# A two-layer fp32 trunk on one core: branch outputs turned by the DMA instead of TensorE, and a rearranged start

## The reference, cut to what matters

```
x = x + 0.5 * swiglu_ffn(rmsnorm(x), w_ffn1_in, w_ffn1_out)        # D_FF 2816
u = rmsnorm(x);  q,k,v,g,p,c,gates = split(u @ w_in)
y_ret  = (retention(q, k, v) * silu(g)) @ w_ret_out                # 4 heads of 128
y_pool = pool_mixer(p) * pool_scale
y_conv = silu(layernorm(depthwise_conv31(a * sigmoid(b)))) @ w_conv_out   # a, b = split(c)
merged = sig(g0)*y_ret + sig(g1)*y_pool + sig(g2)*y_conv
x = x + merged @ w_out
x = x + 0.5 * swiglu_ffn(rmsnorm(x), w_ffn2_in, w_ffn2_out)
```

## Time and profile before

| | us |
|---|---|
| median of 3 runs (range) | 1141.62 (1141.49 to 1142.49) |
| the profiled execution's own time | 1143.67 |
| its span, first to last instruction | 1141.7 |
| PE busy in the span | 1128.9 (99%) |
| DVE busy | 794.9 (70%) |
| ACT busy | 630.0 (55%) |

### The profile page before, as it was taken

How to read it: one execution, slowest core, us unless ns; L and a number is a source line. 1 busy time by engine, 2 the same in 40 slices (tenths; PEclk the granted TensorE clock), 3 DMA queues, 4 the chain that set the end, 5 groups by cost and what they waited for, 6 DMA issues and landing times.

```text
span 1141.7 us, 13153 instructions
## 1 busy us (share of the span) xinstructions
PE 1128.9 (99%) x5063; PEld 931.9 (82%) x5063; DVE 794.9 (70%) x974; ACT 630.0 (55%) x723; POOL 31.5 (3%) x68
## 2 busy tenths in 40 slices
PE   9999999999999999999999999999999999999997
PEld 6788888788878888888888888878888788888886
DVE  5756565799999766555476656477999986665543
ACT  6755536654555675644465554275637366655442
POOL 1000000000100000000000000000001001000000
PEclk9999999999999999999999999999999999999999
DMA  9976665663764586756587656475637646876541
GB/s 348 324 242 219 211 233 160 239 175 139 243 241 151 164 292 212 238 156 230 174 274 250 236 180 233 176 217 207 212 120 261 233 152 184 273 244 210 168 184 37
DMA packets 116078, 240.99 MB, mean 211 GB/s; under 512 B 84256, under 2 KB 85664, under 8 KB 91440
## 3 DMA queue, kind: packets, MB, share of 16 engines
q1 hardware_dynamic: 112512, 232.28, 60.8%
q0 software_dynamic: 1648, 6.06, 1.5%
q10 hardware_dynamic: 1856, 1.81, 0.5%
HBM read 219.16 MB, written 1.05 MB: 193 GB/s over the span
## 4 chain that ended last, share of the span: by engine, by line
PE 86%; DVE 7%; DMA 2%; ACT 2%; issue 2%; SPq 1%; POOLq 0%; DVEq 0%; POOL 0%; ACTq 0%
PE acc L385 28%; PE acc L387 28%; PE acc L386 28%; DVE w_lo L1172 3%; DVE y L1396 1%; DMA raw<-in_weights 1%; PE tr L477 1%; ACT w_hi L770 1%; DMA hT_planes<-h_planes 1%; SPq L708 1%; ACT pin L945 0%; DVE gates L1471 0%; DVE ua L1452 0%; DVE gates L1416 0%; DVE qk L1461 0%
## 5 line engine op out<-in xcount | busy, mean ns | idle before, releaser
L1172 DVE TENSOR_TENSOR w_lo<-raw,w_hi 128x2048 fp32r<-128x2048 f32 (+2 forms) x204 | 444.4, 2211 | 87.7 <-ACT w_hi L770 87.7
L770 ACT CAST w_hi<-raw 128x2048 fp32r<-128x2048 f32 (+2 forms) x204 | 375.2, 1849 | 230.0 <-PE acc L387 221.8
L385 PE MATMUL acc<-w_hi,xT_hi 128*128 128x512 f32 x1152 | 453.1, 393 | 1.3 <-DVE w_lo L1172 1.1
L387 PE MATMUL acc<-w_hi,xT_lo 128*128 128x512 f32 x1152 | 449.3, 390 | 0.0
L386 PE MATMUL acc<-w_lo,xT_hi 128*128 128x512 f32 x1152 | 449.1, 390 | 0.0
L385 PEld LDWEIGHTS acc<-w_hi,xT_hi 128*128 128x128 f32 x1152 | 216.7, 188 | 46.4 <-DVE w_lo L1172 1.5
L387 PEld LDWEIGHTS acc<-w_hi,xT_lo 128*128 128x128 f32 x1152 | 216.7, 188 | 45.6
L386 PEld LDWEIGHTS acc<-w_lo,xT_hi 128*128 128x128 f32 x1152 | 216.9, 188 | 43.9
L1248 DVE SCALAR_TENSOR_TENSOR h<-acc,rs,silu_gate 128x256 f32<-128x256 f32 x88 | 42.5, 483 | 154.7 <-ACT silu_gate L837 154.4
L385 PE MATMUL acc<-w_hi,hT_hi 128*128 128x512 f32 x348 | 135.4, 389 | 0.0
L386 PE MATMUL acc<-w_lo,hT_hi 128*128 128x512 f32 x348 | 135.4, 389 | 0.0
(11 more groups left out here) (138 smaller groups left out, 629.4 us busy)
## 6 DMA issues: line engine op xcount, KB each, us to landing
raw<-in_weights SPq DMA_DIRECT2D x192, 1024.0 KB, 5.0
raw<-in_weights SPq DMA_DIRECT2D x20, 256.0 KB, 7.2
raw<-in_weights SPq DMA_DIRECT2D x8, 512.0 KB, 3.5
bias<-in_gate_bias POOLq DMA_DIRECT2D x6, 512.0 KB, 6.5
x<-in_x SPq DMA_DIRECT2D x2, 512.0 KB, 10.7
hT_planes<-h_planes SPq DMA_TRANSPOSE x64, 3.1
scale_row<-in_pool_scale POOLq DMA_DIRECT2D x2, 512.0 KB, 7.7
x_first<-in_x_first ACTq DMA_DIRECT2D x7, 128.0 KB, 6.0
```

The costliest lines, as they stand in the source:

```text
L385: nc.tensor.matmul(o, a_hi, b_hi, start=first, stop=False)
L387: return nc.tensor.matmul(o, a_lo, b_hi, start=False, stop=last)
L770: nc.scalar.copy(w_hi[:, hf % HIGHS, 0:n], raw[:, hf % RAWS, 0:n]).then_inc(hi_split, 1)
L1172: nc.vector.tensor_tensor(w_lo[:, hf % RAWS, 0:n], raw[:, hf % RAWS, 0:n], w_hi[:, hf % HIGHS, 0:n].bitcast(F32), ALU.subtract).then_inc(l ...
```

## The change

- `u` and `merged` are no longer transposed by PE. ACT splits them into planes, SP issues a DMA transpose; for `u` ACT joins (`u_out`), for `merged` DVE joins into `mT_whole` (`merged_join`), from which ACT makes the high and DVE the low part. PE waits for `merged_lo_ready` ahead of each of the four pieces of M_OUT. The planes of both use buffers that q/k and the retention output had used.
- The four turnings of `merged` stand in SP's order right behind the load of half 2*FFN2, ahead of the next two loads.
- At the start, steps 3 to 7 of x are loaded on SP's queue, each ahead of its quarter of weights, DVE makes the first high part of x, 10 warm-up matmuls are left of 11, and `par` and `ident` are loaded later. Two instructions of the first FFN block change places on ACT.
- Five of the 124 taps move from the retention stage to the pool stage, and `ret_low(0)` between two `sub`.

```
-            keep_busy(11)
+            keep_busy(10)
...
-                wide(l, M_CONV, M_CONV, 1, side, range(4), True, True,
-                     {(0, 1): lambda: turn_merged(l, 0, 0), (1, 1): lambda: turn_merged(l, 0, 1)})
-                wait_tr_taken(pe, ("m", l, 0, 0))
-                wide(l, M_OUT, M_OUT, 0, xT, range(4), True, False,
-                     {(0, 2): lambda: turn_merged(l, 1, 0), (1, 1): lambda: turn_merged(l, 1, 1)})
...
+                wide(l, M_CONV, M_CONV, 1, side, range(4), True, True)
+                for t in range(T):
+                    for c in (0, 1):
+                        pe.wait_ge(merged_lo_ready, 4 * l + 2 * t + c + 1)
+                        wide(l, M_OUT + c, M_OUT, t, xT, range(4 * c, 4 * c + 4), c == 0, c == 1)
...
+            def turn_u(l, t):                                          # SP
+                sp.wait_ge(u_split, l * T + t + 1)
+                sp.dma_start_transpose(...).then_inc(u_turned[t], 16)
...
+            def turn_merged(l, t, c):                                  # SP
+                sp.wait_ge(merged_split, 4 * l + 2 * t + c + 1)
+                if t:
+                    sp.wait_ge(merged_joined, 4 * l + c + 1)
+                sp.dma_start_transpose(...).then_inc(merged_turned[c], 16)
...
+                if 3 <= i < KT:                                        # SP, ahead of quarter i
+                    load_first_x(sp, i)
...
+                if hf % HALVES == 2 * FFN2:                            # SP, behind the load of hf
+                    for t in range(T):
+                        for c in (0, 1):
+                            turn_merged(l, t, c)
...
+            def split_merged(l, t, c):                                 # ACT
+                act.wait_ge(merged_all, 4 * l + 2 * t + c + 1)
+                act.wait_ge(merged_turned[c], 16 * (2 * l + t))
+                nc.scalar.copy(ret_planes[:, c], ...).then_inc(merged_split, 1)
...
+            def merged_join(l, t, c):                                  # DVE
+                dve.wait_ge(merged_turned[c], 16 * (2 * l + t + 1))
+                if t:
+                    dve.wait_ge(merged_lo_ready, 4 * l + c + 1)
+                nc.vector.tensor_copy(mT_whole[:, c, :]..., retT_planes[:, c]
+                                      ).then_inc(merged_joined, 1)
...
                 cast(ahead(M_CONV))                                    # ACT, mixer
+                split_merged(l, 0, 0)
+                split_merged(l, 0, 1)
                 merged_high(l, 0, 0)
+                split_merged(l, 1, 0)
                 cast(ahead(M_CONV) + 1)
+                split_merged(l, 1, 1)
                 merged_high(l, 0, 1)
-
                 merged_high(l, 1, 0)
+                merged_high(l, 1, 1)
                 cast(ahead(M_OUT))
-                merged_high(l, 1, 1)
...
                 merge(l, CONV, 0, 0, merged_all)                       # DVE, mixer
+                sub(l * HALVES + 2 * M_CONV + 4)
                 merge(l, CONV, 0, 1, merged_all)
-                sub(l * HALVES + 2 * M_CONV + 4)
+                merged_join(l, 0, 0)
                 merged_low(l, 0, 0)
+
                 merge(l, CONV, 1, 0, merged_all)
+                merge(l, CONV, 1, 1, merged_all)
+                merged_join(l, 0, 1)
                 merged_low(l, 0, 1)
-
-                merge(l, CONV, 1, 1, merged_all)
                 sub(l * HALVES + 2 * M_OUT + 3)
+                merged_join(l, 1, 0)
                 merged_low(l, 1, 0)
+                merged_join(l, 1, 1)
                 merged_low(l, 1, 1)
                 sub(l * HALVES + 2 * M_OUT + 4)
...
-                subs(M_GATE_POOL + 1)                                  # DVE, pool stage
+                sub(l * HALVES + 2 * (M_GATE_POOL + 1) + 3)
+                conv_taps(l, 2)
+                sub(l * HALVES + 2 * (M_GATE_POOL + 1) + 4)
                 conv_taps(l, 6)
                 gate_z(l, POOLED, 1, 0)
-                conv_taps(l, 9)
+                conv_taps(l, 12)
...
                 gate_z(l, RET, 0, 1)                                   # DVE, retention stage
-                subs(M_GATE_RET + 1)
+                sub(l * HALVES + 2 * (M_GATE_RET + 1) + 3)
+                ret_low(l, 0)
+                sub(l * HALVES + 2 * (M_GATE_RET + 1) + 4)
                 gate_z(l, RET, 1, 0)
-                ret_low(l, 0)
...
-                conv_taps(l, 8)
+                conv_taps(l, 5)
```

More of the change, by code:

```diff
@@ L261, in trunk @@
         u_ready = sem("u_ready")
+        u_split = sem("u_split")
+        u_turned = [sem(f"u_turned{t}") for t in range(T)]
+        u_whole = sem("u_whole")
         pad_zero = sem("pad_zero")
@@ L478, in transpose4, with turn_y @@
                 mm.then_inc(tr_full, 1)
-            def turn_merged(l, t, c):
-                pe.wait_ge(merged_all, l * 4 + 2 * t + c + 1)
-                transpose4(("m", l, t, c), [merged[:, t, c, i * P:(i + 1) * P] for i in range(4)])
-            def turn_u(l, t):
+            def turn_y(l, t):
                 if l == t == 0:
                     pe.wait_ge(ident_landed, 16)
-                pe.wait_ge(u_ready, l * T + t + 1)
-                transpose4(("u", l, t), [ua[:, t, c * P:(c + 1) * P] for c in range(CH)])
-            def turn_y(l, t):
                 pe.wait_ge(conv_step, (l + 1) * CH * TAPS)
@@ L610, in mixer @@
             def mixer(l):
-                two_blocks(l, M_A, 1, {5: lambda: turn_u(l, 0)})
-                in_block(l, M_Q, 0, mid={3: lambda: turn_u(l, 1)})
+                two_blocks(l, M_A, 1)
+                in_block(l, M_Q, 0)
                 in_block(l, M_Q, 1)
@@ L730, in _ @@
                 for t in range(T):
+                    if hf % HALVES == 2 * M_B + t + RAWS:
+                        turn_u(l, t)
                     if hf % HALVES == 2 * M_K + RAWS:
@@ L881, in ffn @@
                 for b in range(2, FB):
+                    if l + f == 0 and b == 4:
+                        act.dma_start(par[:], params.rearrange("l p n -> p l n")
+                                      ).then_inc(par_landed, 16)
+                        act.dma_start(ident, ident_in).then_inc(ident_landed, 16)
                     silu(l, f, b - 1, 1)
@@ L1386, in conv_taps @@
                     else:
-                        for t in range(T):
-                            wait_tr_taken(dve, ("u", l, t))
+                        dve.wait_ge(u_whole, l * T + T)
                     w = PAR_CONV_W + c * TAPS + k
```

115 lines of the change are left out of this document (68 added, 47 removed).

## The result

| | median of runs, us | profiled execution, us | its span, us |
|---|---|---|---|
| before | 1141.82 (1140.84 to 1143.15, 20 runs) | 1143.67 | 1141.7 |
| changed | 1143.84 (1142.55 to 1146.62, 20 runs) | 1144.89 | 1143.1 |

The ratio is 1.0017, interval 1.0010 to 1.0024: the changed kernel is 1.1 to 2.7 us slower, for most of that interval less than the 2.3 us (0.2%) up to which the forecast speaks of no change.

What follows compares the result with a forecast made beforehand. PE's own work and stops were taken to bound the kernel. -3.6 (transposes) - 7.0 (u) - 1.4 (start) - 1.9 (taps) + 14.8 (`merged` waits) = +0.9 us, added to 1141.62, gave 1142.5 us, range 1133 to 1148.5.

Steps and rivals of the forecast that it cites:

- What bounds the kernel: Whole kernel: PE, busy 99% of the span; a change gains what leaves PE's list and stops, little over 15 us at most.
- What leaves PE: Transposes on PE: a group of four costs 0.45 us, so eight groups of `merged` give 3.6 us.
- `turn_u`: u's transposes in both layers: groups, stops and layer 0's low clock go, 7.0 us together, bounds -6 to -7.4.
- The start: First loads and FFN block: -1.4 us, bounds -0.5 to -2.4; early stops go, the third, near 31, gets longer.
- The taps: Retention and conv stages: moving five taps removes PE's short waits for DVE, -1.9 us, bounds -1.0 to -2.1.
- The new path of `merged`: M_OUT and the seam into the second FFN: PE waits 7.4 us a layer, +14.8 in all, bounds 8 to 20.
- The six waits: PE's stops per layer: 0.4, 1.2, 0.85 at M_OUT's pieces, then 0.9, 2.75, 1.2 us in the second FFN's first blocks.
- The sum: Whole kernel: +0.9 us on the span; with the profiled execution's 2.05 us offset from the median kept, 1142.5 us.
- A: M_OUT and seam: ACT and DVE keep up, waits hidden, `merged` path costs only 4 us; 1131.7 us, chance 0.14.
- B: Turnings of `merged` or the seam meet loads in flight, 6.4 instead of 3.1 us; +6, 1148.5 us, chance 0.18.
- C: Seam: part of its delay is taken up, the chain shortens by 2 us a layer; 1138.5 us, chance 0.16.
- D: Start and taps give nothing, the same stops come back one place later; +3.3, 1145.8 us, chance 0.12.

Runs made afterwards that it cites:

- e5: The changed kernel with `merged` turned by PE again, as before; start, u and taps stay changed: 1132.99 us, ratio to the kernel before 0.9918.
- e7: The changed kernel with the order around M_OUT rearranged on both ACT and DVE (merges, high parts, casts, last `sub`): 1137.02 us, ratio to the kernel before 0.9955.
- e2: The kernel before with only u turned by the DMA: 1136.85 us, ratio to the kernel before 0.9953.
- e3: The kernel before with only the start changed (x on the weights' queue, first high part on DVE, `par` and `ident` later): 1140.92 us, ratio 0.9993.
- e12: The kernel before with u turned by the DMA and the taps moved, start and `merged` as before: 1134.99 us, ratio to the kernel before 0.9936.
- e4: The kernel before with only five taps moved to the pool stage and `ret_low(0)` between two `sub`: 1139.97 us, ratio to the kernel before 0.9977.
- e1: The kernel before with only `merged` turned by the DMA, with its order on DVE and ACT: 1151.97 us, ratio to the kernel before 1.0083.
- e9: The changed kernel with the DMA turnings of the second tile's `merged` planes (both halves) done twice in series: 1148.90 us, ratio to the kernel before 1.0058.
- e11: The changed kernel with the last cast on ACT ahead of `merged_high(1,0)` and the last `sub` on DVE ahead of `merged_low(1,1)`: 1139.26 us, ratio to before 0.9973.
- e8: The changed kernel with the first four taps after the second rotary step on DVE instead of ahead of it: 1143.98 us, ratio to the kernel before 1.0014.
- e10: The changed kernel with the DMA turning of `merged`'s first tile, first half, done twice in series: 1150.78 us, ratio to the kernel before 1.0073.

## Why the prediction was right

Point by point, by its own steps.

**What bounds the kernel.** Right: PE is busy 98 to 99% in each kernel and what changes the time is PE's list and its stops. The kernel with the least standing, e5, is the fastest, though e7 and the changed one have less work for PE.

**What leaves PE.** Right. The `merged` stage grew by 5.58 and 5.31 us while its stops and the low clock lost 7.37 and 7.01, so 1.8 and 1.7 us left it, 3.5 where 3.6 were told. PE's busy sum, down 4.3 for twelve groups and one matmul of the warm-up, 0.3 to 0.36 a group, leaves out the late restart behind a group, 0.09, and agrees. The 0.22 worked out from the formula of the Trainium skill (TensorE: Matmul & The Clock Gate, section Back-to-back issue gap) is too low; it is the formula for a matmul by itself, and the same section gives about 81 ns for one of 128 columns in a stream, which would make a group 0.32, an estimate that is too low as well.

**`turn_u`.** In the traces -5.05 and -2.08 against -7.0 in all: right. In the runs -5.4: too large by some 1.6 against the medians. The mistake was to take the low clock of the earlier trace rows as a part of each execution. The prediction had the hint at hand: the profiled execution took 2.05 us more than the median, and I carried this offset over to the changed kernel instead of asking what in the trace was not in the median. "Nothing takes their place that I can find" held in the two stages themselves, but not everywhere behind them: the changed kernel's own trace has the stop of layer 1 (1.2 us), and e2's has two small ones, 1.1 us together.

**The start.** Predicted -1.4. The traces of before and after have -1.56, e3 -0.8, e5 against e12 -2.1, the marks 0.9. The sign is right, the size isn't told any closer, and that the two traces come within 0.2 of the forecast is partly luck: the mark of before, 128.11, is the latest of its five, and e3's stands at 125.78, 2.3 sooner. The stops went otherwise than told: the one ahead of 12.31 became one of 0.54 ahead of 8.77, and the third, near 31, got shorter (0.36 idle) and not longer.

**The taps.** -1.9 predicted, -2.1 by the stages of e4 (-1.05 and -1.0), -2.6 by its runs with an interval that holds 1.9.

**The new path of `merged`.** The six waits were 0.4, 1.2, 0.85, 0.9, 2.75 and 1.2 by the forecast. They came at the forecast places in layer 0, with 0.63, 0.96, 0.82, 0.82 and 2.55 lost, and then eight matmuls at half speed that used up the sixth, 1.6 us for them. In layer 1 the clock stayed up, and the sixth stop is there with 1.25. The stage cost the same in both, +5.58 and +5.31, since the seam's chain and not PE sets its end: this was the sentence "matmuls at half speed then only use up the 1.2 that follows". The windows view of the changed kernel, behind the long stop of layer 0 and of layer 1:
```profile
394.60:397.00 2.40, 2.40 (x7) 0.50 1.09 156
960.00:962.00 2.00, 2.00 (x10) 1.00 1.00 182
```
The seam's first add was forecast 6.6 us late in the time of before, at 387.2; with the changed kernel 7.67 ahead at y's turning that is 379.5, and it came at 379.17. The transposes landed in 3.1. What PE lost in all is 7.37 + 7.01 = 14.4, where 14.8 were told. By the runs of e1 the path costs +9.5 net of the transposes, where 14.8 - 3.6 = 11.2 were told; the interval's upper end is 11.1; by the traces +10.9.

**The sum.** Two errors of the other sign met: the merged path a little cheaper than told, u 1.6 us poorer in the runs. With -5.4 in place of -7.0 the sum would have been +2.5, near the measured +2.0. The two groups of times say the same in another way: among the 20 runs of before beside the changed kernel their means are 1141.3 and 1142.8, and the changed kernel's median is 2.5 above the one and 1.0 above the other. So +0.9 was right for the kind of execution that the trace of before shows, and it was added to a median, 1141.62, of the other kind. That this shift was no larger than 1.7 us, well inside the range, is why the forecast held in spite of it.

**The rivals.** A (waits hidden, 1131.7) fell: they are all there. B (turnings meet loads) fell: the waits for the DMA in the changed kernel are 0.71 a layer, and e9 shows 2 to 3 us in hand at the second tile's. The wait of 3.57 at the seam's first join is the usual 3.1 behind the split (379.89 to 380.94, join at 384.03), no more. C (the seam's chain gets shorter) fell for the kernel as it is, and e7 and e11 show that only another order brings it. D (start and taps give nothing) fell for the taps, and for the start isn't excluded by e3's interval alone.

## What to carry over

To take work off the busiest engine pays only where the way round it is not a chain through engines that already follow each other closely: here 3.6 us of transposes off PE became 14.4 us of waits, while the same edit for u, which nobody near wanted, was worth 5.4 by the runs. Before a stage is rebuilt, write down its chain on the helping engines step by step with measured durations; it told the first late add within 0.4 us, and it shows at once which cast stands in the way (e11: 5 us for two moved lines). And a difference between the profiled execution and the median of the runs is to be explained by the trace, not carried over; look first whether the single times form two groups, and in which of them the profiled execution lies.

## What the runs showed of the hardware

- A stop of PE of 2.1 to 2.5 us brought the lower clock level in some executions and not in others, with the same instructions ahead: for `turn_u` of layer 0 in the trace of before (idle 2.29), not in those of e1, e3 and e4 (2.11, 2.13, 2.25); behind the seam's stop in layer 0 of the changed kernel but not in its layer 1 (2.31 idle in both), and in e8 the other way round (2.30 and 2.31). It lasted eight matmuls, 0.43 us apart, in before and in the changed kernel. In layer 0 of e10, where a stop of 3.56 us stands ahead of M_OUT, it lasted twelve, in layer 1, behind 3.52, eight.
- The DMA transposes of h and x land in 3.0 us at the median in the changed kernel, those of the planes of `merged` and of the retention output in 3.1. Those of u and of q and k, which SP issues among the weights' loads, have a median of 4.3 and a longest of 9.2. The page, DMA issues (tile, queue, kind, count, median us to landing):
```profile
hT_planes<-h_planes SPq DMA_TRANSPOSE x64, 3.0
...
qkT_planes<-qk_planes SPq DMA_TRANSPOSE x12, 4.3
```
